# Cached keys and values loaded from ScalarE's queue instead of SyncE's, in a two-layer hybrid decoder

## The chip, the cores and the metric

The kernel runs on one core of one Trainium2 chip. The metric is the device time of one launch in microseconds; less is better. All arithmetic is in float32.

## What is computed

Two decoder layers run over 288 tokens: a prompt of 256 and 8 sample sequences of 4 new tokens each. Each layer has three token mixers on one input projection (a gated linear recurrence, a state-space recurrence, and attention), a gated merge with an output projection, and a feed-forward part (dense in layer 0, 8 experts in layer 1). The part that matters here is the attention of the sample tokens. It reads cached keys and values of three window groups with dilations 1, 4 and 16:

```python
def dilated_attention_sample(q, k, v, buf, dil):
    wb, S = buf.shape[1], q.shape[1]
    keys = jnp.concatenate([buf[:, :, 0].astype(k.dtype), k], axis=1)
    vals = jnp.concatenate([buf[:, :, 1].astype(v.dtype), v], axis=1)
    idx = wb + jnp.arange(S)[:, None] - dil * jnp.arange(ATT_KEYS + 1)[None, :]
    ...
    s = jnp.einsum('bshd,bsjhd->bshj', q, kg, preferred_element_type=jnp.float32) * ATT_SCALE
    ...
    o = jnp.einsum('bshj,bsjhd->bshd', p, vg) / den
    return o, (m + jnp.log(den))[..., 0]
```

For each layer and each of the 8 sequences the kernel thus fetches one tile of keys and one of values, 9 blocks of up to 128 positions by 256 numbers.

## The kernel before

The program is written by hand as one instruction stream per engine, joined by semaphores. Nothing reorders it: each engine does its instructions in the order of the code, and an instruction that waits holds up all behind it on its engine. SyncE (SP) issues every DMA.

**Banks.** PSUM has 8 banks, and a list of jobs made beforehand says which bank each group of matmuls fills. `filled(key)` is the semaphore by which TensorE (PE) tells that a job is complete, and `drained(key)` the one by which ScalarE (ACT) or VectorE (DVE) tells that it has been copied out. ACT's helper `copy_out` waits for `filled`, copies, raises `drained` and waits for its own copy before it goes on.

**Cache buffers.** `load_cache(L, which, b)` fetches the keys (`which` 0) or values (1) of sequence `b` in layer `L` into `kb[b % 2]`, one of two buffers. It issues three DMAs (lines 549 to 551) of 128, 512 and 256 KB.

**Attention of a layer, first half: keys.** When `ssm_done` is raised (the state-space branch has been normalised), PE turns keys and values of the new tokens into rows (`kvtok`, 9 jobs over five banks, copied out by ACT) and then does rounds `n` = 0 to 8:

```python
for n in range(9):
    if n < 8:
        scores(L, n)
        sample_keys(L, n)
    if n > 0:
        weigh(L, n - 1)
    if n < 8:
        sample_scores(L, n)
```

`scores` is one half-head of the prompt. `sample_keys` waits for the keys of sequence n and transposes them in four jobs `("kT", L, n, k)`; DVE copies jobs 0 and 1 out to `KTb`, ACT jobs 2 and 3. `weigh(n - 1)` transposes the softmax weights of the prompt's previous half-head (job `pt`; one bank for an even half-head, two for an odd one), waits until ACT has copied them to `PT`, and multiplies them with `kvtok`. `sample_scores` multiplies `KTb` with the sample queries: 48 matmuls with few columns. In a round ACT thus does an exp, the two `kT` copies, and the copy or copies of `pt`, in this order.

**Second half: values and output projections.** After the rounds PE does, in this order: the output projection of the first branch in two slabs (`out_slab(0, 0)`, `out_slab(0, 1)`), the sample values `sample_values(L, b)` for b = 0, 1, 2, then `out_slab(1, 0)`, values 3, 4, 5, then `out_slab(1, 1)`, values 6 and 7, and the rest. Each `sample_values` raises `v_used` when it is done with its buffer. ACT has nothing to do in this part until the next normalisation.

**SP's queue.** Weights arrive in slabs of up to 1 MB over a ring of four slots; `weights_until(n)` issues the slabs up to n, and before each it waits until PE is done with the slab that was four before. In attention SP loads the keys, each after `filled(("kT", L, b - 2, 3))`, then values 0 and 1, stores the new keys and values (8 DMAs), and then does

```python
for b in range(2, DB):
    weights_until(out0 + RING + min(2 + (b > 3) + (b > 6), 4))
    sp.wait_ge(v_used, L * (DB - 1) + b - 1)
    load_cache(L, 1, b)
```

so for b = 4 it first issues a slab that waits for `out_slab(1, 0)`, and for b = 7 one that waits for `out_slab(1, 1)`.

Of the kernel before, what the change touches and what calls it, by code (L numbers as in the profile page):

```python
# [15 lines left out]
TP, DB, DS = 256, 8, 4  # L16
# [58 lines left out]
def hybrid_decoder(nc, x_prompt, x_sample, state_hgrn, state_ssm, state_conv, cache_kv_w128, cache_kv_w512,  # L75
# [6 lines left out]
    with ctx:  # L82
# [85 lines left out]
        kb = [view(arena, 4608 + 2304 * i, 9, 256) for i in range(2)]  # L168
# [64 lines left out]
        def at(name, L, k=1):  # L233

            return signals[name], L * PER[name] + k

        def up(name):
# [10 lines left out]
        h0_in = [sem(f"h0_in{i}") for i in range(2)]  # L248
        conv_out = [0] * DEPTH
        v_used, up_exp, up_plus, up_sig, a_ready, lb_exp = map(  # L250
            sem, ("v_used", "up_exp", "up_plus", "up_sig", "a_ready", "lb_exp"))
# [150 lines left out]
        def filled(key):  # L402
            b, n = jobs[key]
            return bank_filled[b], n + 1
# [5 lines left out]
        def psum(key):  # L410
            return bank[jobs[key][0]]
# [107 lines left out]
        def _(sp):  # L519
# [21 lines left out]
                sp.dma_start(h0[j % 2], state_ssm[L, :, 2 * j:2 * j + 2].rearrange("b h p n -> (h p) b n")  # L541
                             ).then_inc(h0_in[j % 2], 16)

            def load_cache(L, which, b):
                dst = kb[b % 2]
                c128 = cache_kv_w128[L, b].rearrange("w two h d -> w two (h d)")
                c512 = cache_kv_w512[L, b].rearrange("(m r) two h d -> m r two (h d)", r=4)
                c2048 = cache_kv_w2048[L, b].rearrange("(m r) two h d -> m r two (h d)", r=16)
                sp.dma_start(dst[:, 0, :], c128[:, which, :]).then_inc(k_in[b % 2], 16)
                sp.dma_start(dst[:, 1:5, :], c512[:, :, which, :]).then_inc(k_in[b % 2], 16)  # L550
                sp.dma_start(dst[0:64, 5:9, :], c2048[:, 0:4, which, :]).then_inc(k_in[b % 2], 16)


            for b, (t0, n) in enumerate(BLK):
                src = x_prompt[0, t0:t0 + n, :] if t0 < TP else x_sample.rearrange("b i d -> (b i) d")
                sp.dma_start(arena[0:n, b * D:(b + 1) * D], src).then_inc(x_in, 16)
# [17 lines left out]
            for L in range(DEPTH):  # L574
                ag = first_slab[L] + NS_HG + NS_SSM

                weights_until(first_slab[L] + RING)
                if L > 0:
                    sp.wait_ge(*filled(("dt", L - 1)))
                    sp.wait_ge(stored, 16 * stores[0])  # L580
                    sp.wait_ge(*filled(("ssm_s", L - 1, 3, 1)))
                sp.dma_start(wdt[:, :, :], w_in[L].rearrange("(k p) n -> p k n", p=P)[:, :, OFF_DT:OFF_DT + SH]
                             ).then_inc(wdt_in, 16)
                sp.dma_start(crows[0:DB * TAIL, :], state_conv[L].rearrange("b j c -> (b j) c")
                             ).then_inc(cstate_in, 16)

                weights_until(ag + 7 + RING + 1)
                sp.wait_ge(*filled(("kdtok", L, 2)))
                load_s0(L, 0)
                load_s0(L, 1)  # L590
                for h in range(HH):
                    weights_until(ag + 8 + h + RING + 1)
                    sp.wait_ge(*drained(("hg_s", L, h, 1)))
                    sp.dma_start(s_hgrn[L, :, h].rearrange("b d v -> d b v"), S0[h % 2]).then_inc(s0_in[h % 2], 16)
                    if h + 2 < HH:
                        sp.wait_ge(s0_in[h % 2], 16 * (4 * L + 2))
                        load_s0(L, h + 2)
                sp.wait_ge(*drained(("hg_st", L)))
                sp.dma_start(p_hgrn[L, 0].rearrange("h d v -> d h v"), st_hg).then_inc(st_out, 16)

                weights_until(ag + 13 + RING + 1)
                sp.wait_ge(*drained(("ctail", L, 0)))
                sp.wait_ge(*drained(("ctail", L, 1)))
                store(p_conv[L, 0], crows[0:3, :])
                store(s_conv[L].rearrange("b j c -> (b j) c"), crows[32:32 + DB * TAIL, :])
                conv_out[L] = stores[0]
                sp.wait_ge(*at("hg_done", L))
                for i in range(2):
                    sp.wait_ge(s0_in[i], 16 * (4 * L + 4))
                load_h0(L, 0)  # L610
                load_h0(L, 1)
                weights_until(ag + 18 + RING + 1)
                sp.wait_ge(*drained(("ssm_st", L)))
                sp.dma_start(p_ssm[L, 0].rearrange("(j e) p n -> (e p) j n", e=2),
                             ssm_st.rearrange("p (j n) -> p j n", j=4)).then_inc(st_out, 16)
                for j in range(4):
                    weights_until(ag + 19 + j // 2 + RING + 1)
                    sp.wait_ge(*drained(("ssm_s", L, j, 1)))
                    sp.dma_start(s_ssm[L, :, 2 * j:2 * j + 2].rearrange("b h p n -> (h p) b n"), h0[j % 2]
                                 ).then_inc(h0_in[j % 2], 16)  # L620
                    if j + 2 < 4:
                        sp.wait_ge(h0_in[j % 2], 16 * (4 * L + 2))
                        load_h0(L, j + 2)

                sp.wait_ge(*at("ssm_done", L))
                for i in range(2):
                    sp.wait_ge(h0_in[i], 16 * (4 * L + 4))
                for b in range(DB):
                    if b >= 2:
                        sp.wait_ge(*filled(("kT", L, b - 2, 3)))  # L630
                    load_cache(L, 0, b)
                for b in range(2):
                    sp.wait_ge(*filled(("kT", L, 6 + b, 3)))
                    load_cache(L, 1, b)
                for i in range(4, 9):
                    sp.wait_ge(*drained(("kvtok", L, i // 3, i % 3)))
                for g, dst in enumerate((p_kv128, p_kv512, p_kv2048)):
                    for b in range(2):
                        if g == 0 and b == 0:
                            continue  # L640
                        r = dst[L, 0].rearrange("w two h d -> w (two h d)")
                        store(r[(b * P if g else 0):(b * P if g else 0) + P, :], kvtok[:, b, g, :])
                for g, dst in enumerate((s_kv128, s_kv512, s_kv2048)):
                    store(dst[L].rearrange("b i two h d -> (b i) (two h d)"), kvtok[0:TS, 2, g, :])
                out0 = ag + NS_AG
                for b in range(2, DB):

                    weights_until(out0 + RING + min(2 + (b > 3) + (b > 6), 4))
                    sp.wait_ge(v_used, L * (DB - 1) + b - 1)
                    load_cache(L, 1, b)  # L650
            weights_until(len(slabs))
            sp.wait_ge(*filled(("wo", 1, KT - 1)))
            sp.dma_start(wr, w_router[0].rearrange("(k p) e -> p k e", p=P)).then_inc(w_router_in, 16)
# [818 lines left out]
        def _(act):  # L1472
# [18 lines left out]
            def copy_out(out, key, src):  # L1491
                act.wait_ge(*filled(key))
                empty(fn(out, src, ACT.Copy), key)
# [99 lines left out]
            def qk_rstd(L, g):  # L1593
# [3 lines left out]
                    empty(fn(qsq[:, k, :], psum(key)[:, 0:T], ACT.Ln, scale=1.0 / 64, bias=eps[:, :]), key)  # L1597
                say(fn(qsq, qsq, ACT.Exp, scale=-0.5), "qk_rstd", L, g + 1)

            def attention(L):  # L1600
                act.wait_ge(*at("ssm_done", L))
                for g in range(AG):
                    for b, (t0, n) in enumerate(BLK):
                        key = ("kvtok", L, g, b)
                        copy_out(kvtok[0:n, b, g, :], key, psum(key)[0:n, :])
                for n in range(9):
                    if n < 8:
                        w = n % 2 + 1
                        act.wait_ge(*at("sc_neg", L, n + 1))
                        v = sc[n % 2].rearrange("p k c -> p (k c)")[:, 0:384 * w]  # L1610
                        c = 4 * (n % 2)
                        say(fn(v, v, ACT.Exp, bias=col[:, c + 1:c + 2], accum_out=col[:, c + 2:c + 3]),
                            "sc_exp", L, n + 1)
                        for k in (2, 3):
                            key = ("kT", L, n, k)
                            copy_out(KTb[:, 256 + 512 * (k - 1):256 + 512 * k], key, psum(key)[:, :])
                    if n > 0:
                        m = n - 1
                        for k in range(m % 2 + 1):
                            key = ("pt", L, m, k)  # L1620
                            copy_out(PT[m % 2][:, k, :], key, psum(key)[:, 0:384])
                        if m % 4 == 3:
                            key = ("att_o", L, m // 4)
                            copy_out(yall[:, 8 + m // 4, 0:TP], key, psum(key)[:, 0:TP])
# [11 lines left out]
                empty(fn(sTs[0:64, 2, :], psum(key)[0:64, 256:384], ACT.Copy), key)  # L1636
                key = ("pN", L)
                copy_out(sTn[0:TS].rearrange("p a r -> p (a r)"), key, psum(key)[0:TS, 0:384])

            def mixer(L):  # L1640
                features_mean(L, 0)
# [825 lines left out]
```

## Time and profile before

| | |
|---|---|
| median of 3 runs | 2858.36 us (2856.25 to 2864.93) |
| profiled execution, its own time | 2860.02 us |
| its span | 2858.2 us |
| PE / ACT / DVE / POOL busy | 94% / 22% / 26% / 5% of the span |
| attention with values, layer 0 | about 492 to 746 us |
| attention with values, layer 1 | about 1519 to 1774 us |

Engine shares are over the whole span, of which the experts of layer 1 (from about 1875 us on) take the larger part. In the rows further down, a line number is one of the program; 1489, 830, 836 and 1854 are helpers through which most instructions of ACT, PE and DVE go, so such instructions are told apart by shape and time. "SPq" rows are DMAs being issued by SP: their duration is that of the issue and not of the transfer.

### The profile page before, as it was taken

How to read it: one execution, taken by the hardware profiler on the slowest of the kernel's cores; microseconds unless marked ns; L12 is line 12 of the kernel's file. 1: busy time of each engine (PE TensorE's matmuls, PEld its weight loads, DVE VectorE, ACT ScalarE, POOL GpSimd, SP SyncE). 2: the span in 40 equal slices, each digit the busy share in tenths (PEclk: the TensorE clock that was granted, in tenths of full speed). 3: DMA queues.
4: the chain of work that ended last, by engine and by line, in shares of the span. 5: the costliest groups of instructions: out<-in, count | busy, mean ns of one | idle time of the engine just before them, and what ended most of it. 6: DMA issues, size and time to landing. Idle time of an engine off the chain costs nothing. (4 is left out here: it accounts for less than half of the span.)

```text
span 2858.2 us, 44924 instructions
## 1 busy us (share of the span) xinstructions
PE 2681.3 (94%) x19936; PEld 1807.2 (63%) x19936; DVE 743.2 (26%) x1212; ACT 619.0 (22%) x955; POOL 148.1 (5%) x157
## 2 busy tenths in 40 slices
PE   7998998999999999979898998699999999999999
PEld 5776666888777777766676887535354453544535
DVE  2263233220111102472322210231403213142222
ACT  3412644110044304233642100100000000000000
POOL 2011011000100000121110001000000000000000
PEclk8998897556899999988886566899999999999999
DMA  4433323213245453323232122099999999999994
GB/s 133 127 98 93 92 89 114 66 60 109 77 114 139 118 142 124 112 89 112 85 114 72 52 90 83 14 392 414 377 358 375 354 359 363 365 365 354 358 371 167
DMA packets 290401, 535.25 MB, mean 187 GB/s; under 512 B 10936, under 2 KB 222010, under 8 KB 273824
## 3 DMA queue, kind: packets, MB, share of 16 engines
q1 hardware_dynamic: 290208, 532.38, 52.6%
q8 instruction: 158, 2.59, 0.4%
q14 instruction: 35, 0.29, 0.0%
HBM read 518.50 MB, written 13.85 MB: 186 GB/s over the span
## 5 line engine op out<-in xcount | busy, mean ns | idle before, releaser
L830 PE MATMUL bank<-mem 128*32 128x256 f32 (+11 forms) x15208 | 1646.3, 438 | 60.4 <-DVE mem L1854 21.8
L830 PEld LDWEIGHTS bank<-mem 128*32 128x32 f32 (+4 forms) x15208 | 1019.0, 138 | 656.5 <-issue 418.5
L830 PE MATMUL bank<-hflat,mem 128*128 128x288 f32 x2944 | 746.9, 416 | 13.2 <-DVE hflat L1864 13.2
L830 PEld LDWEIGHTS bank<-hflat,mem 128*128 128x128 f32 x2944 | 570.2, 195 | 179.7 <-issue 22.6
L1489 ACT ACTIVATE mem<-bank 128x288 f32<-128x288 f32 (+9 forms) x452 | 200.8, 462 | 1269.9 <-PE bank L830 647.1
L1489 ACT ACT_TABLE_LOAD x149 | 191.2, 1283 | 61.3 <-PE bank L830 58.0
L836 PE MATMUL bank<-ident,mem 128*128 128x128 f32 (+5 forms) x742 | 141.2, 346 | 50.6 <-DVE mem L1854 15.0
L1854 DVE TENSOR_TENSOR xT<-xT,bank 128x288 f32<-128x288 f32 x88 | 35.8, 451 | 559.5 <-PE bank L830 559.5
L1489 ACT ACTIVATE mem<-mem 128x1152 f32<-128x1152 f32 (+9 forms) x217 | 158.4, 730 | 83.5 <-DVE mem L1914 37.0
L1854 DVE TENSOR_TENSOR mem<-mem,bank 128x288 f32<-128x288 f32 (+2 forms) x172 | 88.9, 525 | 307.0 <-PE bank L830 221.6
L836 PEld LDWEIGHTS bank<-ident,mem 128*128 128x128 f32 (+5 forms) x742 | 106.2, 187 | 93.4 <-issue 52.1
L1854 DVE TENSOR_TENSOR mem<-mem 128x1152 f32<-128x1152 f32 (+10 forms) x79 | 74.9, 948 | 61.0 <-ACT mem L1489 53.6
L1489 ACT ACTIVATE hflat<-xT 128x1152 f32<-128x1152 f32 x8 | 9.3, 1163 | 375.4 <-DVE xT L1854 375.4
L2409 DVE RECIPROCAL hflat<-hflat 128x512 f32<-128x512 f32 x24 | 80.5, 3353 | 0.8
L1489 ACT ACTIVATE hflat<-bank 128x512 f32<-128x512 f32 (+1 forms) x40 | 19.6, 554 | 244.1 <-PE bank L830 244.1
L764 POOL TENSOR_TENSOR mem<-mem 128x1152 f32<-128x1152 f32 (+1 forms) x16 | 43.2, 2699 | 391.1 <-ACT mem L1489 243.4
L2139 DVE SCALAR_TENSOR_TENSOR mem<-bank,amask 128x384 f32<-128x384 f32 x24 | 13.4, 558 | 185.1 <-PE bank L830 185.1
L2409 DVE RECIPROCAL mem<-mem 128x384 f32<-128x384 f32 x24 | 61.3, 2553 | 0.8
L1858 DVE TENSOR_SCALAR mem<-mem 128x576 f32<-128x576 f32 (+2 forms) x34 | 20.3, 597 | 148.9 <-ACT mem L1489 148.5
L1489 ACT ACTIVATE mem<-mem,col 128x384 f32<-128x384 f32 (+2 forms) x18 | 13.7, 760 | 178.2 <-DVE col L2143 172.9
L830 PE MATMUL bank<-ident,mem 128*32 128x128 f32 (+7 forms) x210 | 29.6, 311 | 17.5 <-DVE mem L2335 9.7
L2408 DVE TENSOR_SCALAR mem<-mem 128x384 f32<-128x384 f32 x24 | 8.5, 356 | 125.7 <-ACT mem L1489 125.7
(181 smaller groups left out, 750.8 us busy)
## 6 DMA issues: line engine op xcount, KB each, us to landing
mem<-in_w_moe_up_dram SPq DMA_DIRECT2D x64, 2048.0 KB, 10.1
mem<-in_w_moe_down_dram SPq DMA_DIRECT2D x56, 2048.0 KB, 10.3
mem<-in_w_moe_up_dram SPq DMA_DIRECT2D x32, 2304.0 KB, 10.3
mem<-in_w_in_dram SPq DMA_DIRECT2D x70, 1024.0 KB, 5.1
mem<-in_w_moe_up_dram SPq DMA_DIRECT2D x16, 1536.0 KB, 8.7
mem<-in_w_ffn_up_dram SPq DMA_DIRECT2D x44, 512.0 KB, 4.9
mem<-in_cache_kv_w_dram SPq DMA_DIRECT2D x32, 512.0 KB, 4.7
mem<-in_w_ffn_down_dram SPq DMA_DIRECT2D x16, 704.0 KB, 4.8
```

What stands on the lines that cost most here:

```text
L764: say(gp.tensor_tensor(kt[:, :, 0:w], hgp[:, 4:8, 0:w], dist[:, :, 0:w], ALU.mult), "lvl_k", L, i + 1)
L830: return mm(out, lhsT, rhs, start=start, stop=stop, skip_group_check=True)
L836: return nc.tensor.transpose(out, in_, ident[0:k, 0:k])
L1489: return nc.scalar.activation(out, in_, f, **kw)
L1854: return ve.tensor_tensor(out, a, b, op)
L1858: say(ve.tensor_scalar(v, v, 1.0, SIG_MAX, ALU.add, ALU.min), name, L, k)
L2139: empty(ve.scalar_tensor_tensor(sc[n % 2][:, k, :], psum(key)[:, 0:384], SCALE, amask[:, w - 1 - k, :], ALU.mult, ALU.add), key)
L2408: lstep(ve.tensor_scalar(x, x, 1.0, None, ALU.add))
L2409: lstep(ve.reciprocal(x, x))
```

## The change

All 96 issues of the cache loads move from SP to ACT, with `load_cache` unchanged but for the engine. The loads of keys 0 and 1 stand ahead of the `kvtok` copies; those of keys 2 to 7 and values 0 and 1 stand in rounds 0 to 7 behind ACT's second `kT` copy and ahead of its `pt` copies; those of values 2 to 7 stand at the end of ACT's attention, each behind its wait for `v_used` alone. SP keeps its slabs, stores and `v_used` waits.

```diff
--- before.py
+++ after.py
@@ SP, in layer L
                 sp.wait_ge(*at("ssm_done", L))
-                for i in range(2):
-                    sp.wait_ge(h0_in[i], 16 * (4 * L + 4))
-                for b in range(DB):
-                    if b >= 2:
-                        sp.wait_ge(*filled(("kT", L, b - 2, 3)))
-                    load_cache(L, 0, b)
-                for b in range(2):
-                    sp.wait_ge(*filled(("kT", L, 6 + b, 3)))
-                    load_cache(L, 1, b)
...
                     weights_until(out0 + RING + min(2 + (b > 3) + (b > 6), 4))
                     sp.wait_ge(v_used, L * (DB - 1) + b - 1)
-                    load_cache(L, 1, b)
@@ ACT
+            def load_cache(L, which, b):
+                dst = kb[b % 2]
...
+                act.dma_start(dst[:, 0, :], c128[:, which, :]).then_inc(k_in[b % 2], 16)
+                act.dma_start(dst[:, 1:5, :], c512[:, :, which, :]).then_inc(k_in[b % 2], 16)
+                act.dma_start(dst[0:64, 5:9, :], c2048[:, 0:4, which, :]).then_inc(k_in[b % 2], 16)
+
             def attention(L):
                 act.wait_ge(*at("ssm_done", L))
+                for i in range(2):
+                    act.wait_ge(h0_in[i], 16 * (4 * L + 4))
+                load_cache(L, 0, 0)
+                load_cache(L, 0, 1)
...
                         for k in (2, 3):
                             key = ("kT", L, n, k)
                             copy_out(KTb[:, 256 + 512 * (k - 1):256 + 512 * k], key, psum(key)[:, :])
+                        if n < DB - 2:
+                            load_cache(L, 0, n + 2)
+                        else:
+                            load_cache(L, 1, n - DB + 2)
...
+                for b in range(2, DB):
+                    act.wait_ge(v_used, L * (DB - 1) + b - 1)
+                    load_cache(L, 1, b)
```

ACT's program in layer 0, from the Exp that ends the state-space normalisation (`128x288`) through the first `kvtok` copies (`128x512`, `32x512`), before the change:

```order
L1489 ACTIVATE mem<-mem 128x288
L1489 ACTIVATE mem<-bank 128x512 x2
L1489 ACTIVATE mem<-bank 32x512
L1489 ACTIVATE mem<-bank 128x512 x2
L1489 ACTIVATE mem<-bank 32x512
```

The same place in the changed program:

```order
L1469 ACTIVATE mem<-mem 128x288
L1585 DMA mem<-in_cache_kv_w_dram 128x256
L1586 DMA mem<-in_cache_kv_w_dram 128x4x256
L1587 DMA mem<-in_cache_kv_w_dram 64x4x256
L1585 DMA mem<-in_cache_kv_w_dram 128x256
L1586 DMA mem<-in_cache_kv_w_dram 128x4x256
L1587 DMA mem<-in_cache_kv_w_dram 64x4x256
L1469 ACTIVATE mem<-bank 128x512 x2
L1469 ACTIVATE mem<-bank 32x512
```

Six DMA issues now stand between `ssm_done` and the first `kvtok` copy. ACT's rounds 1 and 2 before the change (`128x768` and `128x384` with `col` are the exps, `128x512 x2` the two `kT` copies, `128x384` without `col` the `pt` copies):

```order
L1489 ACTIVATE mem,col<-mem,col 128x768
L1489 ACTIVATE mem<-bank 128x512 x2
L1489 ACTIVATE mem<-bank 128x384
L1489 ACTIVATE mem,col<-mem,col 128x384
L1489 ACTIVATE mem<-bank 128x512 x2
L1489 ACTIVATE mem<-bank 128x384 x2
```

And the same two rounds in the changed program:

```order
L1469 ACTIVATE mem,col<-mem,col 128x768
L1469 ACTIVATE mem<-bank 128x512 x2
L1585 DMA mem<-in_cache_kv_w_dram 128x256
L1586 DMA mem<-in_cache_kv_w_dram 128x4x256
L1587 DMA mem<-in_cache_kv_w_dram 64x4x256
L1469 ACTIVATE mem<-bank 128x384
L1469 ACTIVATE mem,col<-mem,col 128x384
L1469 ACTIVATE mem<-bank 128x512 x2
L1585 DMA mem<-in_cache_kv_w_dram 128x256
L1586 DMA mem<-in_cache_kv_w_dram 128x4x256
L1587 DMA mem<-in_cache_kv_w_dram 64x4x256
L1469 ACTIVATE mem<-bank 128x384 x2
```

In each round three issues now stand between the second `kT` copy and the `pt` copies. On SP, in the second half of the attention of layer 0, values 4 and 5 stood behind the second `w_o` slab before the change:

```order
L529 DMA mem<-in_w_o_dram 128x8x256
L549 DMA mem<-in_cache_kv_w_dram 128x256
L550 DMA mem<-in_cache_kv_w_dram 128x4x256
L551 DMA mem<-in_cache_kv_w_dram 64x4x256
L549 DMA mem<-in_cache_kv_w_dram 128x256
L550 DMA mem<-in_cache_kv_w_dram 128x4x256
L551 DMA mem<-in_cache_kv_w_dram 64x4x256
```

There the changed program's SP has only the stores and the slabs:

```order
L534 DMA out_dram<-mem 128x512 x5
L534 DMA out_dram<-mem 32x512 x3
L529 DMA mem<-in_w_out_att_dram 128x2x1024
L529 DMA mem<-in_w_o_dram 128x8x256 x4
L529 DMA mem<-in_w_ffn_up_dram 128x8x128 x44
```

The value loads are no longer behind a slab. The stores are no longer behind the key loads.

## Rows read from the trace of the kernel before

**Rows 1.** The page: busy time of each engine, then the cache's DMA issues

```profile
PE 2681.3 (94%) x19936; PEld 1807.2 (63%) x19936; DVE 743.2 (26%) x1212; ACT 619.0 (22%) x955; POOL 148.1 (5%) x157
...
mem<-in_cache_kv_w_dram SPq DMA_DIRECT2D x32, 512.0 KB, 4.7
```

**Rows 2.** Waits of PE for the cache's transfers, 480 to 1830 us: total, times, longest

```profile
PE bank L830 <- DMA mem<-in_cache_kv_w_dram: 12.2, 4, 3.5
```

**Rows 3.** PE's timeline, values of both layers: start, duration, [idle before, releaser]

```profile
699.02 34.09 PE L830 MATMUL bank<-mem 128*128 128x8 f32 x140 [3.04 <-DMA mem<-in_cache_kv_w_dram]
735.70 9.19 PE L830 MATMUL bank<-mem 128*128 128x8 f32 x36 [2.60 <-DMA mem<-in_cache_kv_w_dram]
...
1726.79 33.99 PE L830 MATMUL bank<-mem 128*128 128x8 f32 x140 [3.52 <-DMA mem<-in_cache_kv_w_dram]
1763.81 9.19 PE L830 MATMUL bank<-mem 128*128 128x8 f32 x36 [3.03 <-DMA mem<-in_cache_kv_w_dram]
```

**Rows 4.** SP's queue, values of layer 1

```profile
1698.50 0.35 SPq L549 DMA_DIRECT2D mem<-in_cache_kv_w_dram  x1
...
1717.41 0.39 SPq L529 DMA_DIRECT2D mem<-in_w_o_dram  x1
1717.84 0.58 SPq L549 DMA_DIRECT2D mem<-in_cache_kv_w_dram  x1
...
1723.30 0.34 SPq L549 DMA_DIRECT2D mem<-in_cache_kv_w_dram  x1
```

**Rows 5.** Start of attention, layer 1, all engines, in order of time

```profile
1519.29 0.36 SPq L549 DMA_DIRECT2D mem<-in_cache_kv_w_dram  x1
1519.35 5.04 ACT L1489 ACTIVATE mem<-bank 128x512 f32<-128x512 f32 x8 [2.37 <-issue]
...
1522.24 0.63 SPq L551 DMA_DIRECT2D mem<-in_cache_kv_w_dram  x1
...
1526.58 2.43 PE L836 MATMUL bank<-ident,mem 128*128 128x128 f32 x18 [1.03 <-DMA mem<-in_cache_kv_w_dram]
1526.85 0.15 DVE L2143 TENSOR_SCALAR col<-col 128x1 f32<-128x1 f32 x1
...
1527.10 0.42 DVE L2148 COPY mem<-bank 128x256 f32<-128x256 f32 x1
```

**Rows 6.** Round 1 of layer 1, all engines, in order of time

```profile
1544.30 0.33 SPq L549 DMA_DIRECT2D mem<-in_cache_kv_w_dram  x1
1544.37 0.60 ACT L1489 ACTIVATE mem<-bank 128x512 f32<-128x512 f32 x1 [0.45 <-PE bank L836]
1544.68 0.55 SPq L550 DMA_DIRECT2D mem<-in_cache_kv_w_dram  x1
1545.20 0.49 ACT L1489 ACTIVATE mem<-bank 128x384 f32<-128x384 f32 x1 [0.24 <-PE bank L836]
1545.27 0.63 SPq L551 DMA_DIRECT2D mem<-in_cache_kv_w_dram  x1
...
1545.79 10.51 PE L830 MATMUL bank<-mem 128*64 128x128 f32 x48 [0.69 <-issue]
```

**Rows 7.** PE's timeline, rounds 2 to 4 of layer 1

```profile
1558.24 3.63 PE L836 MATMUL bank<-ident,mem 128*128 128x128 f32 x18 [0.47 <-DVE mem L2148]
1561.88 10.95 PE L830 MATMUL bank<-mem 128*64 128x128 f32 x60
...
1578.81 10.54 PE L830 MATMUL bank<-mem 128*64 128x128 f32 x48 [0.64 <-ACT mem L1489]
...
1594.92 13.11 PE L830 MATMUL bank<-mem 128*64 128x128 f32 x60
```

**Rows 8.** Windows: length, busy (count) PE PEld DVE ACT POOL, granted clock, DMA share, GB/s

```profile
1564.00:1566.00 2.00, 2.00 (x16) 1.65 (x14) 0.00 (x0) 0.00 (x0) 0.00 (x0) 0.88 0.71 193
1566.00:1568.00 2.00, 2.00 (x17) 1.89 (x17) 0.00 (x0) 0.00 (x0) 0.00 (x0) 0.98 0.00 0
1598.00:1600.00 2.00, 2.00 (x12) 1.94 (x11) 0.00 (x0) 0.23 (x1) 0.00 (x0) 0.50 0.27 52
```

More of the change, by code:

```diff
@@ L542, in load_h0 @@
                              ).then_inc(h0_in[j % 2], 16)
[L544 to L551, printed above, removed]
             for b, (t0, n) in enumerate(BLK):
@@ L1598, in qk_rstd @@
                 say(fn(qsq, qsq, ACT.Exp, scale=-0.5), "qk_rstd", L, g + 1)
+            def load_cache(L, which, b):
+                dst = kb[b % 2]
+                c128 = cache_kv_w128[L, b].rearrange("w two h d -> w two (h d)")
+                c512 = cache_kv_w512[L, b].rearrange("(m r) two h d -> m r two (h d)", r=4)
+                c2048 = cache_kv_w2048[L, b].rearrange("(m r) two h d -> m r two (h d)", r=16)
+                act.dma_start(dst[:, 0, :], c128[:, which, :]).then_inc(k_in[b % 2], 16)
+                act.dma_start(dst[:, 1:5, :], c512[:, :, which, :]).then_inc(k_in[b % 2], 16)
+                act.dma_start(dst[0:64, 5:9, :], c2048[:, 0:4, which, :]).then_inc(k_in[b % 2], 16)
             def attention(L):
                 act.wait_ge(*at("ssm_done", L))
+                for i in range(2):
+                    act.wait_ge(h0_in[i], 16 * (4 * L + 4))
+                load_cache(L, 0, 0)
+                load_cache(L, 0, 1)
                 for g in range(AG):
```

## The prediction

> **What bounds the kernel now.** I read the engine table first: TensorE is busy 94% of the span and ScalarE 22%, so time can only come from gaps of PE, and only be lost by making gaps [rows 1]. Then I took PE's waits in the two attention stages, the only place where the cache is used. Of the cache's transfers it waits 12.2 us in 4 waits in its matmuls [rows 2]; the wait for keys 0 at the start of attention is another 1.03 us in layer 1 [rows 5]. PE's timeline says where: the four long waits, 3.04, 2.60, 3.52 and 3.03 us, all lie in the value half, ahead of values 4 and of values 7 in each layer [rows 3]. The reader is to see in SP's queue why values 4 are late. The load of values 3 goes out at 1698.50, as `sample_values` of 1 frees its buffer; one `sample_values` at the low clock takes 9.2 us (the 36 matmuls of values 7) [rows 3]. PE runs on with values 2, so the buffer for values 4 must be free at about 1698.5 + 9.2 = 1707.7, but its load goes out at 1717.84, right behind the `w_o` slab at 1717.41 that had waited for `out_slab(1, 0)` [rows 4]. It lost 10 us in the queue, and it shares the DMA engines with a 1 MB slab.
>
> Last I read the key half, where the new instructions go. There PE is in a tight exchange with ACT and DVE: it idles 0.69 us before its weighted product in round 1, ACT starts the `pt` copy 0.24 us after becoming free, and PE's product follows at the end of that copy (1545.20 + 0.49 = 1545.69, PE at 1545.79) [rows 6]. So the copy of `pt` ends last there, and ACT has hardly any slack before it, whatever its 22% says.
>
> **Term 1: the four waits of the value half go.** On ACT the load of values 4 waits for `v_used` alone and is issued at about 1707.7. SP's load at 1717.84, beside the slab, was waited for until 1726.79 [rows 3, 4], 8.95 us; by that worst case values 4 are there at 1716.7, before `out_slab(1, 0)` ends. Values 7 likewise go out before `out_slab(1, 1)`. What is late next is values 5: issued when values 3 are done, at 1723.30 [rows 4], and needed one `sample_values` later, at 1732.5. The median of 4.7 us to landing [rows 1] gives 1728 to 1730; with 8.95 us it would be 1732.3, still in time but just. I count the gain in full: 3.04 + 2.60 + 3.52 + 3.03 = **-12.2 us**. ACT idles in this half, so its 36 issues there cost nothing; if they did cost, the next normalisation is tens of microseconds away.
>
> **Term 2: six issues ahead of the `kvtok` copies.** On SP the six take from 1519.29 to 1522.24 + 0.63 = 1522.87, 3.6 us, while ACT begins to copy at 1519.35 [rows 5]. In the changed program ACT does the one and then the other. PE cannot hide it: it needs the banks back for the rest of `kvtok` and for `scores(0)`. Its 1.03 us wait for keys 0 would absorb a part, but DVE's chain (L2143 ends at 1527.00, the copy of the transposed keys starts at 1527.10) is as late as PE, and it moves by the whole 3.6 us [rows 5]. Two layers: **+7.2 us**.
>
> **Term 3: three issues ahead of the `pt` copy in rounds 1 to 7.** SP's three issues take from 1544.30 to 1545.27 + 0.63 = 1545.90, 1.60 us. ACT's second `kT` copy ends at 1544.97; with 0.05 us on either side of the issues it can start the `pt` copy at 1546.65 instead of 1545.20: 1.45 us later, and PE's product with it [rows 6]. In even rounds, with two `pt` copies, PE starts after the first and idles nowhere between transposes and product (1558.24 + 3.63 = 1561.87, product at 1561.88) [rows 7]; the first copy slips by about the same. I take 1.43 us a round, 7 rounds a layer, 2 layers: **+20.0 us**. Round 0 has no `pt` copy and costs nothing.
>
> The trace has no DMA issued by ACT, so the price of an issue there is bounded. From below by nothing, if ACT could hand the work on and go ahead at once: terms 2 and 3 vanish. From above by the longest issue of the rows that carry these terms, 0.63 us, for all of them: three would take 1.97 us with the gaps and six 4.0 us, and terms 2 and 3 would be 8.0 + 14 x 1.80 = 33.2 instead of 27.2. I take SP's own durations, since it is the same three DMAs, and since SP itself starts the next only 0.05 us after the last ended (0.33 from 1544.30, next at 1544.68), so an issue does hold its engine [rows 6].
>
> What the Trainium skill says on this is in "Perfetto Trace Analysis", section "DMA Instruction — HWDGE (DVE, Sync)": the time shown for such an instruction ends when the sequencer is free for the next one, which would hold for ACT as for SP and gives +27.2 us for these terms. Against it stands "DMA: Bandwidth & Descriptors", "Issuing engines are not separate DMA queues", by which issuing from several engines saves a sequencer time that is usually small beside the transfer; read as "issues are cheap" it gives about 0 for them and 2860.0 - 12.2 = 2847.8 in all.
>
> **Term 4: the clock in even rounds.** The product and sample scores of rounds 2 and 6 take 10.95 us, those of round 4 take 13.11 us with the same 60 matmuls [rows 7]. The difference, 2.16 us, is the granted clock: in round 2 it goes from 0.50 (1.2 GHz) to 0.88 and 0.98 (2.4 GHz) for some 4 us, after transposes and product ran without a gap since 1558.24; in round 4 it stays 0.50 [rows 8]. Layer 0 shows the same pattern. No odd round shows a rise; these have 0.64 or 0.69 us of idle in front of the product [rows 6, 7]. After the change every even round gets a gap of 1.4 us at just that place, twice the gap that goes with no rise in the odd ones. So I expect the rises of rounds 2 and 6 to be lost in both layers: 4 x 2.16 = **+8.6 us**. Bounds: -4.3 us (all six even rounds rise, if the shifted phase happens to favour it) and +8.6.
>
> **Covered.** SP's 8 stores of new keys and values move from the end of the key half to its start; nothing waits for them in attention. The key loads of round n+2 go out some 0.7 us later than on SP, behind ACT's copy rather than with it, and are needed over 20 us later against 4.7 us to landing [rows 1, 7]. If this cover were gone PE would wait as it does for values 4, some 3 us each.
>
> **The sum.** -12.2 + 7.2 + 20.0 + 8.6 = +23.6 us, on the profiled execution's own 2860.0: 2883.6. That execution is 1.7 us above the median of the runs, 2858.4, so the forecast is 2858.4 + 23.6 = **2882 us**, 0.8% slower.
>
> **Rivals.** All against the median.
> - Clock kept. Terms 1 to 3 hold and some or all of the rises survive, or others come: +15.0 us, 2873.4; down to +10.7, 2869.1, if all six even rounds rise. For it: which rounds rise depends on phase as well (round 4 does not). Against: the gap. Chance 0.22.
> - Issues dearer on ACT. At 0.63 us each it is +29.6 us, 2888. Chance 0.13, up to some 2894 if values 5 also come late for part of term 1.
> - Not slower: ACT's issue does not hold the engine. Its place is between `kT` and `pt` copies. With g us for a group of three, a round costs g - 0.17 (the 0.24 us that ACT waited anyway, less 0.05 and the change of handover), the start of attention 2g; 14(g - 0.17) + 4g = 12.2 gives g = 0.81, half of what SP needs. Below that the gain wins; at g = 0 the time is 2846. Only SP's rows speak on this, and against. Chance 0.08 for faster; 0.05 for the strip within 0.3%, which also holds g near 1.
> - The change does not do what it says: values 4 and 7 stay late, because three transfers on ACT's queue and slabs on SP's share the same engines. Then +35.8, 2894. Against: by the worst row, values 4 land 1 us before they are needed, and the slab is issued only later. Chance 0.05.
>
> The forecast itself has 0.47; its own range is 2877 to 2887 (0.1 us on each issue's handling, one rise kept).
>
> **How the numbers follow.** About 0.3%, 8.6 us, is what a measurement of this kernel can tell from no change. Slower by more than that: 0.47 + 0.22 + 0.13 + 0.05 = 0.87. The range for 8 in 10 must take in the clock rival and the dearer issues: 2868 to 2892.
>
> **What will show it.** In the changed profile: DMA issues on ACT of 0.33, 0.55 and 0.63 us; ACT's first `kvtok` copy 3.6 us after `ssm_done`; PE idle of about 2.1 us before the product in odd rounds and 1.4 us in even ones, put down to ACT; the granted clock 0.50 all through rounds 1 to 7, and products of even rounds of 13.1 us; no wait for the cache in the value half. The prediction is wrong if PE's gaps before the product stay under 1 us (issues are cheap), or if PE waits for values 5.

## The result, and the profile after

The changed kernel takes 2889.94 us (median of 4 runs, 2886.34 to 2891.67), the kernel before, run beside it, 2861.32 us. The ratio is 1.010 with a 95% interval of 1.0078 to 1.0121: slower by 1.0%, or 28.6 us. The profiled execution takes 2891.2 us with a span of 2889.5, which is 31.3 us more than the span of before.

The page of the changed kernel begins as follows: busy time by engine, and the cache's issues, which are now ACT's.

```profile
PE 2696.5 (93%) x19936; PEld 1815.4 (63%) x19936; DVE 743.2 (26%) x1212; ACT 619.0 (21%) x955; POOL 148.1 (5%) x157
...
mem<-in_cache_kv_w_dram ACTq DMA_DIRECT2D x32, 512.0 KB, 4.6
```

Busy time hides the loss: ACT's is 619.0 us as in [rows 1], since issues are not counted as busy. PE's waits from 480 to 1870 us show it (total, times, longest). The first line is from before, the other two are from the changed kernel:

```profile
PE bank L830 <- ACT mem L1489: 23.1, 20, 3.6
...
PE bank L810 <- ACT mem L1469: 47.9, 27, 6.0
PE bank L816 <- DVE mem L2148: 12.2, 16, 1.2
```

No wait for the cache is left, against 12.2 us in [rows 2], and the wait for ACT has doubled. The start of attention in layer 1, all engines, answers to [rows 5]:

```profile
1537.42 0.34 ACTq L1585 DMA_DIRECT2D mem<-in_cache_kv_w_dram  x1
...
1540.33 0.65 ACTq L1587 DMA_DIRECT2D mem<-in_cache_kv_w_dram  x1
1541.03 4.35 ACT L1469 ACTIVATE mem<-bank 128x512 f32<-128x512 f32 x7 [5.97 <-issue]
1541.68 1.91 PE L810 MATMUL bank<-ident,mem 128*32 128x128 f32 x8 [5.65 <-ACT mem L1469]
...
1545.42 1.92 PE L810 MATMUL bank<-ident,mem 128*32 128x128 f32 x8
...
1549.95 0.42 DVE L2148 COPY mem<-bank 128x256 f32<-128x256 f32 x1
```

The six issues hold ACT from 1537.42 to 1540.98, and PE idles 5.65 us. (A turned tile below is a transposed one: the turned keys are `kT`, the turned weights `pt`.) The transposes of `kvtok` then stay slow: the eight of the row at 1545.42 take 1.92 us, the same eight before the change 1.06. Round 1 of the same layer answers to [rows 6]:

```profile
1566.36 0.60 ACT L1469 ACTIVATE mem<-bank 128x512 f32<-128x512 f32 x1 [0.45 <-PE bank L816]
1566.98 0.33 ACTq L1585 DMA_DIRECT2D mem<-in_cache_kv_w_dram  x1
1567.35 0.56 ACTq L1586 DMA_DIRECT2D mem<-in_cache_kv_w_dram  x1
1567.94 0.65 ACTq L1587 DMA_DIRECT2D mem<-in_cache_kv_w_dram  x1
1568.64 0.49 ACT L1469 ACTIVATE mem<-bank 128x384 f32<-128x384 f32 x1 [1.68 <-issue]
...
1569.23 10.50 PE L810 MATMUL bank<-mem 128*64 128x128 f32 x48 [2.14 <-issue]
```

The three issues fill the time between the copy of the turned keys and that of the turned weights, and the gap ahead of PE's product is 2.14 us instead of 0.69. An even round and the value half of layer 1, in PE's timeline, answer to [rows 7] and [rows 3]:

```profile
1586.75 13.09 PE L810 MATMUL bank<-mem 128*64 128x128 f32 x60 [1.45 <-ACT mem L1469]
...
1624.86 13.09 PE L810 MATMUL bank<-mem 128*64 128x128 f32 x60 [1.46 <-ACT mem L1469]
...
1709.06 93.86 PE L810 MATMUL bank<-mem 128*128 128x288 f32 x396
```

All even rounds take 13.09 us, and the value half is one piece of 396 matmuls without a gap.

To see where the 31.3 us went I cut the span at three landmarks in each layer: the end of DVE's last `ssm_done` multiplication (key half begins), the start of the eight transposes of `pN` (value half begins), the start of the third branch's product (value half ends). All in us, from profiles; "between" lies between the value half of layer 0 and the key half of layer 1 and is the same program in all kernels.

| profile | key half, layers 0 and 1 | value half | between | after that |
|---|---|---|---|---|
| before | 151.7, 151.9 | 102.2, 102.9 | 773.3 | 1084.1 |
| before, second execution | 151.7, 152.0 | 102.3, 103.0 | 777.1 | 1081.3 |
| changed | 171.0, 170.6 | 96.1, 96.1 | 777.9 | 1085.5 |
| changed, second execution | 170.9, 170.6 | 96.1, 96.1 | 777.8 | 1085.5 |

The key halves lose 19.3 and 18.7 us, the value halves gain 6.1 and 6.9, together +25.0 us. The other 6.3 us lie outside the stages that were edited: 4.6 between, 1.4 after, 0.3 ahead of the attention of layer 0.

### The profile page after: what moved, and what is told of

It reads as the page before. It is cut to its first block and busy times, and to the rows that moved or that the text cites. A ratio compares the mean times of both kernels' runs of the same rounds, so it can differ in the third digit from the quotient of the medians.

```text
span 2889.5 us, 44918 instructions
## 1 busy us (share of the span) xinstructions
PE 2696.5 (93%) x19936; PEld 1815.4 (63%) x19936; DVE 743.2 (26%) x1212; ACT 619.0 (21%) x955; POOL 148.1 (5%) x157
## 5 line engine op out<-in xcount | busy, mean ns | idle before, releaser
L1858 DVE TENSOR_SCALAR mem<-mem 128x576 f32<-128x576 f32 (+2 forms) x34 | 20.3, 598 | 148.5 <-ACT mem L1469 148.2
L1469 ACT ACTIVATE mem<-mem,col 128x384 f32<-128x384 f32 (+2 forms) x18 | 13.7, 761 | 185.9 <-DVE col L2143 180.6
L810 PEld LDWEIGHTS bank<-ident,mem 128*32 128x32 f32 (+8 forms) x210 | 21.4, 130 | 33.2 <-issue 16.8
```

The source lines that it names most:

```text
L810: return mm(out, lhsT, rhs, start=start, stop=stop, skip_group_check=True)
L1469: return nc.scalar.activation(out, in_, f, **kw)
L1858: say(ve.tensor_scalar(v, v, 1.0, SIG_MAX, ALU.add, ALU.min), name, L, k)
```

## The experiments

Us beside a ratio are the ratio less one, times 2861. "SP" and "ACT" in a diff stand for the engine whose program it is, and the definition of `load_cache` on the engine that needs it is left out. Each profile is of one execution.

**The value half alone.**

```diff
@@ SP
                     sp.wait_ge(v_used, L * (DB - 1) + b - 1)
-                    load_cache(L, 1, b)
@@ ACT, end of attention
+                for b in range(2, DB):
+                    act.wait_ge(v_used, L * (DB - 1) + b - 1)
+                    load_cache(L, 1, b)
```

> Only the loads of values 2 to 7 are on ScalarE, keys and values 0 and 1 stay on SyncE. Theory (the gain is the slab ahead of values 4 and 7 in SyncE's queue, and ScalarE has nothing queued there): the four waits of 3.04, 2.60, 3.52 and 3.03 us vanish, 12 to 13 us faster than before, about 0.45%. Rival (the transfers themselves are late, sharing the DMA engines with slabs): 3 us or less faster, PE still waits for the cache.

Ratio 0.9969 (0.9958 to 0.9981), 8.9 us faster (5.4 to 12.0). The value halves take 96.4 and 96.3 us in its profile, and PE waits nowhere in them. The rival falls. But the gain is some 3 us less than the waits, and the interval does not reach the 12 to 13 us expected. In this profile, layer 0's key half takes 155.3 us instead of 151.7, with one wait of 2.9 us for keys 0 there, but it also begins 4.6 us earlier (487.5 against 492.1) and ends 0.9 us earlier. What the profile lacks lies in the stretch between, 778.7 us instead of 773.3.

**The same gain without ScalarE.** Here SP's loop only has its lines in another order:

```diff
@@ SP
-                    weights_until(out0 + RING + min(2 + (b > 3) + (b > 6), 4))
                     sp.wait_ge(v_used, L * (DB - 1) + b - 1)
                     load_cache(L, 1, b)
+                    weights_until(out0 + RING + min(2 + (b > 3) + (b > 6), 4))
```

> Everything stays on SyncE; only the order there is changed: the load of each of values 2 to 7 stands ahead of the weight slab and not behind it. Theory (the gain of the change is an order in a queue and not the second queue): 12 to 13 us faster than before, like the kernel that has values 2 to 7 on ScalarE. Rival (a second queue is needed, because slabs of 1 MB in the same queue still delay the cache): under 6 us faster.

Ratio 0.9974 (0.9963 to 0.9984), 7.4 us faster (4.6 to 10.6). This lies between the 12 to 13 us of the theory and the rival's 6, so the stages have to decide: the value halves take 96.4 us each, as with values on ACT, and PE waits nowhere in them. SP's queue in the value half of layer 0 shows values 4 ahead of the slab, and PE's timeline no gap:

```profile
680.02 0.35 SPq L549 DMA_DIRECT2D mem<-in_cache_kv_w_dram  x1
...
689.40 0.39 SPq L529 DMA_DIRECT2D mem<-in_w_o_dram  x1
695.61 0.33 SPq L549 DMA_DIRECT2D mem<-in_cache_kv_w_dram  x1
```

```profile
644.36 94.17 PE L830 MATMUL bank<-mem 128*128 128x288 f32 x396
```

Values 4 go out 9.4 us ahead of the slab. So the change's gain is an order in a queue. A second queue is not needed for it. What the time lacks is again in the stretch between, 778.8 us.

**The start of attention alone.** Keys 0 and 1 are issued by ACT behind `ssm_done`, all else by SP.

```diff
@@ SP
-                for b in range(DB):
-                    if b >= 2:
-                        sp.wait_ge(*filled(("kT", L, b - 2, 3)))
+                for b in range(2, DB):
+                    sp.wait_ge(*filled(("kT", L, b - 2, 3)))
                     load_cache(L, 0, b)
@@ ACT
                 act.wait_ge(*at("ssm_done", L))
+                for i in range(2):
+                    act.wait_ge(h0_in[i], 16 * (4 * L + 4))
+                load_cache(L, 0, 0)
+                load_cache(L, 0, 1)
```

> Only the loads of keys 0 and 1 are on ScalarE, ahead of its copies of the new keys and values. Theory: ScalarE is held 3.6 us by six issues, and PE, idle longer there, does the rest of that part at the low clock, so that the first scores are ready 4.8 us later per layer, as in the changed kernel: +9.6 us. Rival (the wait for keys 0 hides a part of it, and the clock is as before): 2 x 2.6 = +5.2 us.

Ratio 1.0028 (1.0016 to 1.0039), 8.0 us slower. The key halves take 155.6 and 155.2 us, 3.9 and 3.3 more than before. The time lies between the two expectations, and the interval (4.6 to 11.2 us) holds both.

**Half of the rounds each.** Of the loads in rounds 0 to 7, the even (then the odd) rounds' are issued by ACT in the changed kernel's place, and SP keeps the others.

```diff
@@ SP
-                for b in range(DB):
...
+                load_cache(L, 0, 0)
+                load_cache(L, 0, 1)
+                for n in range(1, DB, 2):
+                    sp.wait_ge(*filled(("kT", L, n, 3)))
...
@@ ACT, behind the copies of kT
+                        if n % 2 == 0:
+                            if n < DB - 2:
+                                load_cache(L, 0, n + 2)
+                            else:
+                                load_cache(L, 1, n - DB + 2)
```

> Only the loads behind the turned keys of rounds 0, 2, 4 and 6 are on ScalarE, the others stay on SyncE. Theory (gap of 1.45 us a round, and the rise of the clock in rounds 2 and 6 is lost): 6 x 1.45 + 4 x 2.16 = +17.3 us, products of rounds 2, 4 and 6 at 13.1 us. Rival (only the time of the issues counts, the clock is a matter of phase): +8.7 us, and products of 10.9 us stay in some even rounds.

Even rounds: ratio 1.0048 (1.003 to 1.0067), 13.7 us slower. Each gap is 1.45 us, which makes 8.7. The time lies between theory and rival, its interval (8.6 to 19.2 us) holds both, and the profile shows something of each. Most even rounds take 13.09 us, but round 4 of layer 1 takes 9.38 and round 6 11.01:

```profile
1614.00:1615.00 1.00, 1.00 (x6) 0.84 (x4) 0.00 (x0) 0.46 (x1) 0.00 (x0) 0.50 0.00 0
1615.00:1616.00 1.00, 0.24 (x2) 0.00 (x0) 0.00 (x0) 0.00 (x0) 0.00 (x0) 0.92 0.37 94
1616.00:1618.00 2.00, 1.31 (x12) 1.28 (x12) 0.00 (x0) 0.98 (x2) 0.00 (x0) 1.00 0.81 264
1618.00:1620.00 2.00, 2.00 (x17) 1.76 (x15) 0.00 (x0) 0.38 (x1) 0.00 (x0) 1.00 0.55 148
...
1650.00:1652.00 2.00, 2.00 (x11) 2.00 (x10) 0.00 (x0) 0.14 (x1) 0.00 (x0) 0.50 0.98 306
1652.00:1654.00 2.00, 2.00 (x15) 1.61 (x13) 0.00 (x0) 0.00 (x0) 0.00 (x0) 0.82 0.05 11
```

The first four windows are of round 4, where PE is idle from 1615.24 to 1616.69 (columns as in [rows 8]). The clock rises as the transposes end, just ahead of the gap (0.50 until 1615, 0.92 in the next microsecond), and stays at 1.00 through it. The last two are of round 6, whose product starts at 1649.67 behind the same gap: the clock is 0.50 through the gap and rises some 3 us into the product. Neither way does a gap forbid the rise, as I had put it.

> Only the loads behind the turned keys of rounds 1, 3, 5 and 7 are on ScalarE. Theory (a gap in odd rounds costs its own length alone, rises in even rounds need only that these run without a gap): 8 x 1.45 = +11.6 us, with rises still in four of the six even rounds, give or take one (2.2 us) for the shifted phase. Rival (any shift in the stage kills the rises): +20 us.

Odd rounds: ratio 1.004 (1.0026 to 1.0054), 11.4 us slower (7.4 to 15.4), against 11.6 expected; the rival's 20 is out. The profile does not fit as well. Two of its six even rounds are short, where four, give or take one, were expected, and its key halves lose 8.8 and 8.7 us. It is of the slowest of five executions (2887.0 us, the others 2871.8 to 2876.9), so how many are short in the others is not known.

**The same three issues behind the copies of the turned weights.** The changed kernel, with one block moved:

```diff
@@ ACT, round n: from behind the copies of kT to the end of the round
-                        if n < DB - 2:
-                            load_cache(L, 0, n + 2)
-                        else:
-                            load_cache(L, 1, n - DB + 2)
...
                             copy_out(yall[:, 8 + m // 4, 0:TP], key, psum(key)[:, 0:TP])
+                    if n < DB - 2:
+                        load_cache(L, 0, n + 2)
+                    elif n < DB:
+                        load_cache(L, 1, n - DB + 2)
```

> The changed kernel, but in rounds 0 to 7 the three issues stand behind the copy of the turned weights instead of ahead of it. Theory (the issues cost only where TensorE waits for what is behind them): the gaps before the products are 0.6 and 0 us again, the rises of the clock return, and what stays is the head (+9.6 us) against the value half (-13 us): 0 to 8 us faster than before, some 33 us faster than the changed kernel. Rival (an issue on ScalarE costs wherever it stands, because it holds that engine): as slow as the changed kernel, +28 us.

Ratio 0.9967 (0.9955 to 0.998), 9.4 us faster than before (5.7 to 12.9, where 0 to 8 was expected) and so about 38 us faster than the changed kernel. The rival falls. Its round 1 of layer 1, ACT and PE:

```profile
1552.83 0.49 ACT L1469 ACTIVATE mem<-bank 128x384 f32<-128x384 f32 x1 [0.24 <-PE bank L816]
1553.35 0.34 ACTq L1585 DMA_DIRECT2D mem<-in_cache_kv_w_dram  x1
1553.42 2.77 PE L810 MATMUL bank<-mem 128*64 128x128 f32 x12 [0.69 <-issue]
```

The copy starts 0.24 us after ACT is free and PE's gap is 0.69 us, both as before [rows 6], with the same 96 issues on ACT. Five of its six even rounds are short.

The next one is the same, with keys 0 and 1 issued by SP again:

```diff
@@ SP
                 sp.wait_ge(*at("ssm_done", L))
+                for i in range(2):
+                    sp.wait_ge(h0_in[i], 16 * (4 * L + 4))
+                load_cache(L, 0, 0)
+                load_cache(L, 0, 1)
@@ ACT
                 act.wait_ge(*at("ssm_done", L))
-                for i in range(2):
-                    act.wait_ge(h0_in[i], 16 * (4 * L + 4))
-                load_cache(L, 0, 0)
-                load_cache(L, 0, 1)
```

> As the kernel with the issues behind the copy of the turned weights, and the loads of keys 0 and 1 on SyncE again. Theory: no issue stands ahead of anything that TensorE waits for, so the whole gain of the value half is left, 12 to 13 us faster than before. Rival (issues on ScalarE still cost in rounds): less than 5 us faster.

Ratio 0.9963 (0.9949 to 0.9977), 10.6 us faster (6.6 to 14.6), which holds the 12 to 13 expected and not the rival's 5. Key halves 152.0 and 151.9 us, as before; value halves 96.4 and 96.4. Its interval and that of the kernel above overlap, so the timing does not show the price of the start; the stages do (155.6 and 153.4 us in the kernel above, with one more short round in its layer 1).

**The changed kernel with values 2 to 7 on SP in the old place** (all keys, and values 0 and 1, stay on ACT).

```diff
@@ SP
                     sp.wait_ge(v_used, L * (DB - 1) + b - 1)
+                    load_cache(L, 1, b)
@@ ACT
-                for b in range(2, DB):
-                    act.wait_ge(v_used, L * (DB - 1) + b - 1)
-                    load_cache(L, 1, b)
```

> The changed kernel with the loads of values 2 to 7 back on SyncE in their old place. Theory (the two parts add up): the changed kernel plus the 13 us of the value half, about +42 us against before, TensorE waiting four times for the cache again. Rival (the value half gains less than 13 us once keys are on ScalarE): +30 us.

Ratio 1.015 (1.0134 to 1.0167), 42.9 us slower, as the theory had it; PE's waits have the cache again:

```profile
PE bank L821 <- DMA mem<-in_cache_kv_w_dram: 14.0, 4, 4.1
```

Start (8.0), even (13.7) and odd rounds (11.4) alone add up to 33.1, some 10 us less than all together. All six even rounds take 13.1 us here, while the profiles of the parts alone keep four short ones (start), two and one (even) and two (odd). But 10 us is at the edge of what the intervals of the four times can tell, some 9 us together.

**ScalarE held by something else.** The kernel before, with all loads on SP, and two copies of dead data (`hflat` is free in attention) where the changed kernel has its issues:

```diff
@@ ACT, behind the copies of kT
+                        if n > 0:
+                            step(fn(hflat[:, 0:1152], hflat[:, 0:1152], ACT.Copy))
+                            step(fn(hflat[:, 1152:1408], hflat[:, 1152:1408], ACT.Copy))
```

> The kernel before, with every load on SyncE, but in rounds 1 to 7 ScalarE does two needless copies, together about 1.6 us, where the changed kernel has its three issues; they copy dead data onto itself, so the result is the same. Theory (the price is the time that ScalarE is held between the copies of the turned keys and the turned weights, whatever holds it): gaps of 1.5 us more in rounds 1 to 7 of both layers and most rises of the clock lost, +21 to +35 us. Rival (it is the loads themselves that cost, being late or on a second queue): the loads are as before here, so under +10 us.

Ratio 1.0111 (1.0094 to 1.0128), 31.8 us slower. Round 2 of layer 1, ACT, and rounds 2 to 4, PE:

```profile
1572.06 1.61 ACT L1489 ACTIVATE hflat<-hflat 128x1152 f32<-128x1152 f32 x2
1573.70 1.01 ACT L1489 ACTIVATE mem<-bank 128x384 f32<-128x384 f32 x2
```

```profile
1574.24 11.05 PE L830 MATMUL bank<-mem 128*64 128x128 f32 x60 [1.44 <-ACT mem L1489]
...
1592.72 10.59 PE L830 MATMUL bank<-mem 128*64 128x128 f32 x48 [2.08 <-ACT mem L1489]
...
1610.32 13.15 PE L830 MATMUL bank<-mem 128*64 128x128 f32 x60 [1.44 <-ACT mem L1489]
```

The gaps are the changed kernel's to 0.05 us, with no load moved. So it is the time that ACT is held at this place, whatever holds it. Two of the six even rounds are short in spite of the gap, and in both the clock is 0.50 through the gap and rises some 3 us into the product. The profile is of the fastest of four executions (2883.0 us, the others 2892.3 to 2893.2).

**Second executions.** Three kernels were profiled once more.

> The changed kernel once more, for a second profile. Theory (a gap of 1.45 us ahead of the product keeps the clock down): the products of all six even rounds take 13.1 us again. Rival (the clock is a matter of how the execution falls): some even rounds at 9 to 11 us, as four of six before.

All six products of even rounds take 13.09 or 13.10 us again (own time 2892.12 us).

> The kernel with the loads of rounds 0, 2, 4 and 6 on ScalarE once more, for a second profile. Its first one had two products of 9.4 and 11.0 us behind gaps of 1.45 us. If a gap only makes a rise rarer, again none to two of six are short, not the same ones of need; if the first profile was the same program giving the same pattern, again rounds 4 and 6 of layer 1.

Only round 6 of layer 0 is short this time, behind the same gap:

```profile
572.88 13.09 PE L831 MATMUL bank<-mem 128*64 128x128 f32 x60 [1.45 <-ACT mem L1490]
...
609.57 10.94 PE L831 MATMUL bank<-mem 128*64 128x128 f32 x60 [1.45 <-ACT mem L1490]
```

> The kernel before once more, for a second profile. If rises fall as the execution does, three to five of the six even rounds are short, and the stretch between the two attention stages (773.3 us in the first profile) may differ by some us; if they are fixed by the program, rounds 2 and 6 of both layers are short again and the stretch is 773.3.

Four of six are short again, but in layer 1 rounds 2 and 4 instead of 2 and 6. The stretch between the attention stages takes 777.1 us instead of 773.3. The two executions part in layer 1's mixer, at the same instructions; the first fence is the first execution (PE's timeline), the second the second:

```profile
1337.81 1.24 PE L830 MATMUL bank<-mem,pairs 128*128 128x288 f32 x4
...
1369.71 2.10 PE L830 MATMUL bank<-mem,ones 128*128 128x288 f32 x8
```

```profile
1339.78 2.29 PE L830 MATMUL bank<-mem,pairs 128*128 128x288 f32 x4
...
1373.85 2.21 PE L830 MATMUL bank<-mem,ones 128*128 128x288 f32 x8
```

The `pairs` products ran at the high clock once and not the other time, and by the `ones` products 4.1 us had gone. The kernel had not changed. PE's waits in the stretch do not explain it: 2.4 us in the first execution, 1.9 in the second and slower one.

Over all profiles of these kernels, an even round's product is short (9.4 to 11.1 us instead of 13.1) in 30 of 48 cases where nothing is inserted ahead of its `pt` copies, and in 5 of 36 where the 1.45 us gap is. Odd rounds never show it.

## Why the prediction was right, and where its sizes were off

The forecast was +23.6 us and 2882 us, the range 2868 to 2892; measured were +28.6 us beside before, and 2889.9. The direction, the mechanism and the range held. The time lies in the upper end of the range, though, outside the forecast's own 2877 to 2887 and nearest to the rival of dearer issues (2888), which the rows refute: an issue on ACT takes what it took on SP. Of the 7.9 us above 2882, 3.0 are that before itself took 2861.3 us in the runs beside and not 2858.4.

**Term 1, the value half (-12.2 us).** Right: the profile shows -6.1 and -6.9, and no wait for values 4, 5 or 7. The reordered SP queue shows it was the slab ahead of the load.

**Term 2, the six issues at the start (+7.2 us).** The issues took 3.6 us, but the DVE copy of the turned keys moved from 7.83 us behind `ssm_done` (1527.10 - 1519.27) to 12.61 (1549.95 - 1537.34), 4.8 us. The difference is PE at the low clock, behind an idle time of 5.65 us instead of 2.05. Part came back in round 0, whose sample scores took 9.0 us instead of 9.9, so that the start alone costs 3.3 to 3.9 us a layer, close to the 3.6 forecast, though not for the reason given.

**Term 3, three issues a round (+20.0 us).** Right: the gaps went from 0.69 to 2.14 us and from nothing to 1.45, 14 x 1.45 = 20.3. That an issue on ACT takes as long as on SP is shown by the rows (0.33, 0.56 and 0.65 us, each starting 0.04 us or less after the last ended), and that the place decides by the kernel with the issues behind the copy. By the Trainium skill, "Perfetto Trace Analysis", section "DMA Instruction — HWDGE (DVE, Sync)", the end of an issue's row is when its sequencer is free, and the trace agrees: ACT's next copy starts 0.05 us after it. The Trainium skill, "DMA: Bandwidth & Descriptors", section "Issuing engines are not separate DMA queues", says that the time to initiate a DMA is usually small beside the DMA itself. The trace agrees here too (0.33 to 0.65 us against a median of 4.6 us to landing), but that does not make it cheap: PE waited for the issuer and not for the transfer.

**Term 4, the clock (+8.6 us).** The size was right for this kernel: no even round is short, in either execution. The reason was put too hard. I said a gap loses the rise; it makes it rare, 5 of 36 against 30 of 48. In four of the five the clock rose only some 3 us into the product, in one just ahead of the gap. Why the changed kernel and the one with all key loads on ACT have none in three profiles, where those with half of the gaps, and the one with copies in place of issues, have one or two in each, is not settled. So whether none in this kernel was to be expected, or was luck, stays open.

**What the sum left out.** The edited stages in the profile give +25.0 us, 1.4 above the sum. That is the last product of the key half (24 matmuls in round 8): 4.24 and 4.22 us instead of 3.48 and 3.53, a clock that does not rise there either. Gaps (20.3), even rounds (8.6) and this (1.45) leave 7.6 us of the 38.0 for the two starts, against 7.2 in term 2.

Most of the other 6.3 us is in the stretch between (4.6 us) and the part after the value half of layer 1 (1.4 us). In each layer the third branch's product and the `w_o` slabs take longer in both executions of the changed kernel: 46.33 against 45.00 us in layer 0, 47.35 against 45.83 in layer 1. In layer 1 the clock falls to 0.50 at 1821 us behind PE's short waits for POOL; before it stayed at 1.00. The step that failed is thus that only the attention stages can change: a shift also changes where the clock rises and falls later.

The rest of the stretch between is mostly luck of the profile that I started from. In three of all 14 profiles (the first of before, the start alone, ACT held by copies) two of the six `pairs` products take 1.24 us and none of the others less than 2.2, and just these three have 773.3 us between. The other eleven have 777.0 to 780.5. Against the second execution of before, the changed kernel loses 0.8 us there and not 4.6.

The same holds on the other side. The three kernels that insert nothing in the key half (values on ACT, the reordered SP queue, and issues behind the copy with keys 0 and 1 on SP) gain 12.4 us in the value half by their profiles and 7.4 to 10.6 us in time; their stretch between takes 778.7 to 779.2 us, 1.6 to 2.1 more than in the second execution of before. Some 1.2 us of that is in one run of 704 matmuls of layer 0's feed-forward part (173.8 to 174.0 us against 172.65 in both executions of before). But two profiles of kernels whose value half is as before (the first with even rounds on ACT, and that with odd rounds) take 174.0 there as well, and 780.5 in all. Whether it is a loss that the shift brings or the luck of executions stays open.

## What to carry to other kernels

An engine that is 22% busy can still be the one that ends a wait: before giving it DMA issues, look at what stands behind the place in its stream and who waits for it, and put the issues behind that instruction (here a move behind the next copy or two is worth 38 us, over eight rounds in each of two layers). A load that comes late in a queue may only need to stand ahead of a neighbour that waits longer; the reordered SP queue gained as much, within the intervals, as the second queue did at its best. No kernel here beats before by more than 0.4%; the lowest ratio was that of the kernel with issues behind the copy and keys 0 and 1 on SP, 0.9963, but its interval overlaps those of the three others that gain.

## What the runs showed of the hardware that was not expected

- The same program, executed twice, had its clock rise in different places: 4.1 us of difference in one stretch of 50 us, where PE waited 2.4 us in the faster execution and 1.9 in the slower. A single profile as baseline can thus be lucky by 4 us.
- Behind a gap of 1.45 us between transposes and product, the product took its full 13.1 us in 31 of 36 cases. In four the clock rose from 0.50 some 3 us into the product, and in one it had risen just ahead of the gap and stayed at 1.00 through it.
